# Two transformer blocks on one Trainium2 core: another order for the head norms at the end of the mLSTM

## The reference

```python
h = rms_norm_2(x, mix_norm[l])
z = h @ w_in[l] + b_in[l]
a_q, a_k, a_v, m_q, m_k, m_v, m_o, m_i, m_f, g_pre = jnp.split(z, SPLIT_POINTS, axis=-1)
y_attn = sliding_window_attention(...) @ w_proj_attn[l]
...
hm = mlstm_chunkwise(mq, mk, mv, softcap(m_i), softcap(m_f))      # 8 heads x 128
hm = rms_norm_2(hm, mlstm_head_norm[l]).reshape(b, s, SZ_MV)      # norm over each head's 128
hm = (jax.nn.sigmoid(m_o) * hm)
y_mlstm = hm @ w_proj_mlstm[l]
gates = jax.nn.sigmoid(g_pre).reshape(b, s, 2, D_MODEL)
merged = gates[:, :, 0] * y_attn + gates[:, :, 1] * y_mlstm
x = x + merged @ w_out[l]
```

## Time and profile before

| | |
|---|---|
| median of 3 runs | 1046.1 us |
| lowest, highest | 1045.12, 1046.26 us |
| span of the profiled execution | 1044.0 us |
| PE busy | 1009.9 us (97%) |
| DVE busy | 554.4 us (53%) |
| ACT busy | 425.8 us (41%) |
| POOL busy | 50.9 us (5%) |

### The profile page before, as it was taken

The page is one execution under the profiler, slowest core; times in us unless marked ns, Lnnn a source line. Parts: engine busy times, 40 slices in busy tenths (PEclk is TensorE's granted clock), DMA queues, the critical chain, the costliest instruction groups (busy, mean ns, idle before and its releaser), DMA issues.

```text
span 1044.0 us, 13151 instructions
## 1 busy us (share of the span) xinstructions
PE 1009.9 (97%) x5259; PEld 768.1 (74%) x5259; DVE 554.4 (53%) x847; ACT 425.8 (41%) x566; POOL 50.9 (5%) x60
## 2 busy tenths in 40 slices
PE   8999989999999899999999999999979999999997
PEld 7877876644443358888888899877868888888885
DVE  5677572222222255454455585686766665554453
ACT  5564342222221144344344355574453354434342
POOL 3330000000000000000000000000200010000000
PEclk9999999999999999999999999999989999999998
DMA  8963679999999958565554546422265546555541
GB/s 298 325 212 141 254 291 368 390 420 421 421 421 422 417 159 277 179 199 181 186 196 162 185 158 222 155 88 101 83 207 174 162 147 236 164 197 186 177 160 41
DMA packets 97452, 239.59 MB, mean 229 GB/s; under 512 B 7170, under 2 KB 52314, under 8 KB 82042
## 3 DMA queue, kind: packets, MB, share of 16 engines
q1 hardware_dynamic: 95482, 229.57, 60.3%
q0 software_dynamic: 1920, 9.33, 2.6%
HBM read 237.81 MB, written 3.43 MB: 231 GB/s over the span
## 4 chain that ended last, share of the span: by engine, by line
PE 83%; DVE 8%; DMA 3%; ACT 2%; SPq 2%; issue 1%; POOL 0%; ACTq 0%; POOLq 0%; DVEq 0%
PE banks L1146 20%; PE banks L1148 19%; PE banks L1147 19%; PE banks L1456 6%; PE banks L1483 4%; PE banks L1467 3%; PE banks L1435 2%; DMA stage<-in_w_up 2%; SPq L464 2%; DVE weights_lo L1933 2%; PE banks L1163 1%; PE banks L1310 1%; PE banks L1580 1%; PE banks L1340 1%; DMA raw_weights<-in_ffn_w_up 1%
## 5 line engine op out<-in xcount | busy, mean ns | idle before, releaser
L1933 DVE TENSOR_TENSOR weights_lo<-raw_weights,weights_hi 128x2048 fp32r<-128x2048 f32 x115 | 263.1, 2290 | 155.1 <-ACT weights_hi L727 154.8
L727 ACT ACTIVATE weights_hi<-raw_weights 128x2048 fp32r<-128x2048 f32 x115 | 219.7, 1913 | 149.8 <-PE banks L1148 132.9
L1146 PE MATMUL banks<-weights_hi,normed_T_hi 128*128 128x512 f32 (+1 forms) x624 | 249.8, 400 | 7.6 <-DVE weights_lo L1933 6.0
L1148 PE MATMUL banks<-weights_hi,normed_T_lo 128*128 128x512 f32 (+1 forms) x624 | 243.0, 389 | 0.0
L1147 PE MATMUL banks<-weights_lo,normed_T_hi 128*128 128x512 f32 (+1 forms) x624 | 242.4, 388 | 0.0
L1146 PEld LDWEIGHTS banks<-weights_hi,normed_T_hi 128*128 128x128 f32 x624 | 118.2, 189 | 34.8 <-DVE weights_lo L1933 7.9
L1148 PEld LDWEIGHTS banks<-weights_hi,normed_T_lo 128*128 128x128 f32 x624 | 117.8, 189 | 25.0
L1147 PEld LDWEIGHTS banks<-weights_lo,normed_T_hi 128*128 128x128 f32 x624 | 118.2, 189 | 21.6
L1146 PE MATMUL banks<-weights_hi,ffn_hidden_T_hi 128*128 128x512 f32 x160 | 62.4, 390 | 0.0
L1148 PE MATMUL banks<-weights_hi,ffn_hidden_T_lo 128*128 128x512 f32 x160 | 62.3, 389 | 0.0
L1147 PE MATMUL banks<-weights_lo,ffn_hidden_T_hi 128*128 128x512 f32 x160 | 62.2, 389 | 0.0
(11 more groups left out here) (376 smaller groups left out, 1585.6 us busy)
## 6 DMA issues: line engine op xcount, KB each, us to landing
raw_weights<-in_w_in SPq DMA_DIRECT2D x37, 1024.0 KB, 4.8
raw_weights<-in_ffn_w_gate SPq DMA_DIRECT2D x44, 512.0 KB, 3.7
raw_weights<-in_ffn_w_up SPq DMA_DIRECT2D x44, 512.0 KB, 4.7
raw_weights<-in_ffn_w_down SPq DMA_DIRECT2D x22, 1024.0 KB, 4.7
stage<-in_w_down SPq DMA_DIRECT2D x14, 1024.0 KB, 13.6
expert_weights<-in_w_gate SPq DMA_DIRECT2D x12, 1024.0 KB, 13.4
expert_weights<-in_w_up SPq DMA_DIRECT2D x12, 1024.0 KB, 15.4
expert_weights<-in_w_down SPq DMA_DIRECT2D x12, 1024.0 KB, 16.1
```

The costliest lines, as they stand in the source:

```text
L727: ins = eng.activation(w_hi[:, slot, :], raw, ACT.Copy)
L1146: eng.matmul(dst, x[0], w[0], start=first_one, stop=False)
L1148: return eng.matmul(dst, x[1], w[0], start=False, stop=last_one)
L1933: ins = eng.tensor_tensor(w_lo[:, slot, :], raw, w_hi[:, slot, :], ALU.subtract)
```

## The change

DVE: `rsqrt` goes; `normed_rows(t)` is cut into `row_squares(t)`, which sums the squares and asks for the root, and `normed_rows(t, root)`, which waits for the root and applies it. Between the two of a tile now stands other work: for tile 0 `mlstm_rows(1)`, the split of piece G0 + 6 and tile 1's `row_squares`; for tile 1 tile 0's `normed_rows` and the split of piece G0 + 7. `add_bias(2)` comes behind the split of piece G0 + 8. ACT: `sigmoids(1)` goes ahead of the high half of piece G0 + 7, the squares of tile 1 behind it; `sigmoids(2)` goes behind the high half of piece G0 + 8. PE, POOL and SP have the same programs as before.

```diff
@@ ACT
             feed(G0 + 3)
             squared_rows(0)
             feed(G0 + 4)
-            squared_rows(1)
             sigmoids(1)
             feed(G0 + 5)
+            squared_rows(1)
+            feed(G0 + 6)
             sigmoids(2)
-            feed(G0 + 6)
             feed(G0 + 7)
             feed(first["w_proj_attn"])
             sigmoids(3)
@@ DVE
-            def rsqrt(dst, sums, n):
-
-                roots[0] += 1
-                eng.tensor_scalar(dst, sums, 1.0 / n, EPS, ALU.mult, ALU.add).then_inc(root_in, 1)
-                eng.wait_ge(root_out, roots[0])
-
@@
-            def normed_rows(t):
+            def row_squares(t):
                 eng.wait_ge(ml_hsq, t + 1)
                 link(eng.tensor_reduce(hs[:, t, 3, 0:8], head_squares.rearrange("p (h v) -> p h v", h=8), AX_X, ALU.add))
-                rsqrt(hs[:, t, 3, 8:16], hs[:, t, 3, 0:8], V_DIM)
+                roots[0] += 1
+                eng.tensor_scalar(hs[:, t, 3, 8:16], hs[:, t, 3, 0:8], 1.0 / V_DIM, EPS, ALU.mult, ALU.add).then_inc(root_in, 1)
+                return roots[0]
+
+            def normed_rows(t, root):
+                eng.wait_ge(root_out, root)
                 rows = tok[:, t, :].rearrange("p (h v) -> p h v", h=8)
@@
             mlstm_rows(0)
             feed(G0 + 3)
-            normed_rows(0)
+            first_root = row_squares(0)
+            mlstm_rows(1)
             feed(G0 + 4)
-            mlstm_rows(1)
-            normed_rows(1)
+            second_root = row_squares(1)
+            normed_rows(0, first_root)
             feed(G0 + 5)
+            normed_rows(1, second_root)
+            feed(G0 + 6)
             add_bias(2)
-            feed(G0 + 6)
             feed(G0 + 7)
```

## The result

The changed kernel takes 1037.16 us (median of 4 runs, 1036.64 to 1038.52) against 1046.18 (1045.12 to 1046.27, the three runs from above and one more): a ratio of 0.9914 with a 95% interval of 0.9903 to 0.9926. The forecast was 1037.5 with a range of 1036.7 to 1040.1. The profiled execution has a span of 1035.1 us instead of 1044.0.

The account below looks back on a forecast made before the run. PE, busy 97% of the span, was taken as the bound, stopped before piece 7 by DVE's order. Gains of 0.11, 0.15, 5.51 and 2.81, about 8.6 us off 1046.1, gave 1037.5 us, range 1036.7 to 1040.1.

Parts of the forecast that it names:

- The sum: PE never waiting for pieces 6 and 7 gains 0.11, 0.15, 5.51 and 2.81 us, together 8.58 us.
- What held piece 7: Before piece 7, the order of DVE's program, not data, was said to hold PE back, 5.5 us.
- DVE's new order: On DVE, splits of pieces 7, 8 and 9 were to end at 759.3, 763.9 and 769.9.
- The margins: DVE's splits were to end ahead of PE's need by 1.7 us for piece 7, 2.0 us for piece 9.
- The tie at tile 1's squares: ACT ends tile 1's squares at 753.27, DVE comes at 753.25; ACT lateness delays DVE equally, 1.7 us free.
- Transfers: Loads of weight pieces 8 to 11 were all to land before they are wanted; no load becomes the late one.
- POOL: Tile 1's root, asked for at 754.7 and wanted at 759.2, takes 1.65 or 2.65 us; no cost taken.
- Rival 1: Tile 1's root waits until DVE halts, making pieces 8 and 9 late: 1038.6 us, up to 1040.1; chance 0.13.
- Rival 2: Later stages paced by DMA give the gain back: 0 to 3 us left, 1043 to 1046; chance 0.04.
- Rival 3: DVE still waits for tile 1's squares from ACT; with 2 us over the margin, 1042.3 us; chance 0.03.
- Rival 4: Slower: a late tile 1 root holds up DVE's longer queue; landing at 769 gives 1048.1 us; chance 0.05.
- Rival 5: The new order leaves PE's wait where it is: same time as before, 1046.1 us; chance 0.01.

Follow-up runs that it names:

- experiment 1: Changed kernel with ACT's old order, and add_bias(2) back ahead of the split of piece G0 + 8: 1038.64 us, ratio to before 0.9926.
- experiment 2: Kernel before with only the ACT lines of the change: 1046.96 us, ratio 1.0005.
- experiment 5: Changed kernel with one more sum of tile 1's squares on DVE behind tile 1's root request: 1038.16 us.
- experiment 6: Changed kernel with three more sums of tile 1's squares on DVE behind tile 1's root request: 1039.18 us.
- experiment 4: Changed kernel with tile 1's squares on ACT ahead of sigmoids(1) and the high half of piece 7: 1039.58 us, ratio 0.9933.
- experiment 3: Changed kernel, but DVE waits for each root as soon as it has asked for it: 1040.85 us, ratio 0.9943.

## Why the prediction was right

- **The sum.** 8.58 us were forecast from four differences. The tail is 8.66 us shorter (298.53 - 289.87), and piece 8 starts at 766.21 on a time base that is 0.24 us earlier than before's, where 766.46 was worked out. The medians differ by 9.0, the rest being that 0.24 and the spread of the runs. That the median came within 0.4 us of the forecast is partly luck: the four runs spread over 1.9 us, and the same kernel run again had 1038.22.
- **What held piece 7.** Named from the chain of waits: DVE's order. Experiments 1 and 2 show it: DVE's part alone removes the stop, ACT's part alone leaves it at 5.34 us.
- **DVE's new order.** Laid out from the durations of before it gave an end of the split of piece 7 at 759.3, of piece 8 at 763.9, of piece 9 at 769.9; measured, with the 0.24 added, 759.3, 763.9 and 769.9. The margins, 1.7 and 2.0, are 1.70 and 1.99, and experiments 5 and 6 bracket the first.
- **ACT.** The tie at tile 1's squares held, the sum starting at 753.05, 0.04 us behind where DVE's split let it; experiment 4 shows that giving the squares the front place would change nothing either way. The prediction gave the move of `sigmoids(2)` behind piece 8 no share of its own; experiment 1 gives it 1.5 us.
- **Transfers.** No wait of PE for a DMA came up.
- **POOL: the one length off.** The prediction took 1.65 us for tile 1's root, 2.65 at worst, and the root took 2.49. It cost nothing, since it ended at 757.11 and DVE came for it at 758.99. Rival 1 had assumed that the root gets no turn until DVE halts. It got one while DVE was busy, since the second product and the split followed on the first without a pause. What it waited for was the end of the instruction that DVE was in: the first product ended at 755.60 and the root 1.5 us later. The same holds elsewhere in the traces. In the kernel before, the second of two roots began inside a split that ended at 55.13 and ended at 56.63, again 1.50 later. In the execution of experiment 4 one took 3.03 us, and it too ended 1.50 us after its split (43.83 + 2.29 = 46.12, 44.59 + 3.03 = 47.62):

```profile
43.83 2.29 DVE L1927 TENSOR_TENSOR weights_lo<-raw_weights,weights_hi 128x2048 fp32r<-128x2048 f32 x1 [4.35 <-ACT weights_hi L727]
44.59 3.03 POOL L597 TENSOR_TENSOR head_stats<-head_stats,minus_half 128x8 f32<-128x8 f32 x1
```

  So 2.65, the longest row of one trace, was not a bound. An estimate from these rows is the end of the split or product that the root begins in, plus 1.5 us; here 755.60 + 1.5 = 757.1. The other half of the rule that the prediction cites from the Trainium skill (page "SBUF — State Buffer", section "Who interferes with whom"), that whichever came first keeps the shared port pair to its end, does not show on DVE's side: in experiment 5 the product that began at 755.82, inside the root that ran from 754.81 to 756.46, took its usual 1.23 us.
- **Rivals 2 to 5** did not come: PE's waits behind piece 6 are the three that were there before, none of them for a DMA, and DVE stands idle neither at tile 1's sum nor at its products. Rival 4 needed the root to land at 767.0; it landed ten us earlier.
- **The restart price.** Rival 3 allowed the clock to fall after a stop of 2 us. Experiments 3 and 6 stopped PE for 2.00 and 1.95 us and it did not fall, in one execution each; at 4.45 us it did.

## What to carry to other kernels

When the engine at the bound waits for a hand-written queue of another engine, lay that queue out from measured durations and ask of each entry whether the bound waits for it: requests go early, and their answers are fetched behind the work that the bound wants next. Give each such piece a margin in us and know it; here 1.7 us decided between no cost and a full one. When a step is moved on one engine (`add_bias(2)` on DVE), ask whether its partner on the other (`sigmoids(2)` on ACT) has to move with it; here one without the other would have made the two wait for each other, by their order in the program (not run). To compare variants of a late stage, subtract what lies ahead of it: tails that should be equal came out within 0.1 us (289.9 four times) or 0.2 (298.5 and 298.3), where medians of one kernel moved by 1.

## What the runs showed of the hardware that I had not expected

- A root of 128 x 8 values on POOL took 1.65 us beside DVE's one-input sum and 2.49 beside its two-input product, with DVE equally busy in both and its product no slower (1.22 us). One that began inside a split or a product ended about 1.5 us after that instruction, up to 3.03 us long in the rows shown.
- What a stop costs PE behind it is not one number. Piece 7 took 5.44 us without a stop, 0.1 to 0.2 more after 1.95 and 2.00 us with the clock at 1.00, 1.5 more after 4.45, 2.6 more after 5.34 (experiment 2) and 2.8 more after 5.36; one profiled execution each.
- One stretch far from the change (150 to 155 us, behind a row of short waits in the routing) is granted the full clock in six of the ten profiled executions and about three quarters of it in four, though the program is the same there. PE's longest wait from 130 to 160 us is 1.1 us in executions of both kinds, so the length of a single stop does not decide it; what does stays open. That alone moves all behind it by 1.4 to 1.5 us, as much as several of the effects measured here.
